# Waits of a two-block network on one core: orders of exponentials, scaled keys, tables, scalings and norms changed

## Chip, cores and metric

One core of a Trainium2 chip. The metric is the device time of one execution in microseconds, the median of several runs; the profile comes from one further execution.

## What is computed

Two blocks of two layers each, width 1024, 256 tokens (the first block has a second sequence of 256 context tokens), all in float32. The output is that of the last layer of the second block. Cut to what matters:

```python
# first block, layer 0 (even) and 1 (odd)
h = h + 0.5 * m[2] * swiglu(modulate(rmsnorm(h)), ffn1)     # 1024 -> 2 x 2816 -> 1024
h = h + m[5] * mixer(modulate(rmsnorm(h)))   # layer 0: wkv scan in both directions; 1: depthwise conv 31 + pools
h = h + 0.5 * m[8] * swiglu(modulate(rmsnorm(h)), ffn2)
# the scan of layer 0, for both sequences and both directions
sk = S @ kk[t]; S = S * w[t] - sk b[t]^T + v[t] k[t]^T; y[t] = S @ r[t]
# second block: layer_norm(alpha * x + (1 + gate) * f(modulate(x))), f = swiglu, mixer, swiglu
# mixer of layer 0: RG-LRU (linear recurrence over time) beside gated linear attention in chunks of 64
# mixer of layer 1: latent attention
cq, ckv, k_pe = split(u @ w_in); q = rms_norm(cq) @ w_q_up; kv = rms_norm(ckv) @ w_kv_up
q_pe, k_pe = rope(q_pe), rope(k_pe); o = softmax(causal(q k^T)) v; return o @ w_out
```

## The kernel before

All five engines run one long program each, written out by hand; semaphores tie them together. Activations lie as columns of features by 256 tokens (X, Y), weights come in chunks of 256 columns into two buffers W[0] and W[1] (SyncE issues their transfers; `free(c)` waits until chunk c-2 has been used), and products go to four PSUM banks in turn, each of which ScalarE or VectorE must empty (semaphore `s_ev`) before it is used for the fourth tile after. `phases` gives the order of stages: the first FFN F[0], the rwkv mixer, F[1], F[2], the conv mixer, F[3], F[4], the gated linear attention ("gla"), F[5], F[6], the latent attention ("mla"), F[7], with norms between them.

**FFNs F[1] to F[7]** (`small_ffn`, one on each engine) do each pair of 2 x 128 gate and up columns as seven products of half size (L2522; the down columns L2562) instead of eight, with sums of weight blocks (S1 to S4: L2841, L2846, L2850, L2855) and of token blocks (L2864 to L2871) on VectorE. In a pair u ScalarE copies the first product to C1 (L2641), which TensorE's second product in the same banks waits for, takes the silu S0 (L2645) and, when VectorE has the sum, the silu C12 (L2647). In F[4] to F[7] ScalarE runs `norm_scale` (L1555, eight activations on X) at the start of u=1; VectorE waits for it (`s_xa`) before the down columns. Before F[1] ScalarE takes the silu of the rows c (CB, L2711), which VectorE needs for the modulation products (`ada`, L2754), in F[1] from pair 2 on; VectorE waits for it (`s_sc` 4) before the token sums of F[1].

**The scan of rwkv** (`rwkv_scan_pe`, `_act`, `_dve`, `_pool`) takes chunks n = 0 to 3 for one sequence and 4 to 7 for the other; the heads are in two halves t = 0, 1. Within a chunk a chain of small products (64 x 64) goes back and forth between TensorE and the engines that empty and mask its banks. For the next chunk ScalarE computes exponentials (`exps`, L861 to L864, and `inverse_exps`, L873, into KH), GpSimd multiplies them with keys (`keys`, L1136 and L1139; `inverse_keys`, L1146 and L1147, into BH and KH), TensorE forms `first_b` (L654) and `first_a` (L640, L643) and VectorE masks them (L1022, L1017). ScalarE's order in a chunk: the copies of turned keys KHT and BHT (L907, L908) for t=0 and 1, the copies VT1 and VT0 of turned values (L911, L915) for t=0 and 1, then `inverse_exps` for t=0 and 1, then the copies GG and UU1 (L877). TensorE's: turned values (L664), Q2 products, then for each t the product that needs VT0 and, where there is a next chunk, its `first_b`; then for each t the product with GG and `first_a`. In the second sequence VectorE does bonus products (L1076 to L1079) before it masks `first_b`.

**Conv and gla.** `first` makes SyncE wait (conv: for the end of the FFN before; gla: for the last modulation group) and issue five transfers of small tables (conv: the pool weights, L1334, and the pool table, 1 MB, L1336; gla: L1544, L1545) before the first weights of the mixer (L2364). In the gla mixer VectorE needs, for the recurrence (L1814) the factor TH (1 + TH, L1803, reciprocal, L1804, product, L1805, then ScalarE's Sqrt, L1745) and, for the attention, the scaled QD, KI and KE (L1807 to L1809), without which TensorE's `scores` (L1613) don't start. After them come SCO cleared (L1810), AI (L1812), the recurrence, the masks (L1822), the copies KET (L1828) and the states (L1833 to L1836).

**The mla mixer** projects to three tiles of latents CQ and one of keys KP (L604, copies L2024, L2026), squares the three (L2029), sums them (L1926), takes two roots (L2032), reciprocals (L2094) and norms (L2097), and multiplies up (L1941 queries, L1951 and L1956 keys and values). The angles' sine tables (L2052, L2053) come after the value copies, and VectorE waits for them before the rotation (L2103 to L2116).

## Time and profile before

| | |
|---|---|
| runs | 3156.06 us median of 3 (3154.03, 3156.06, 3161.24) |
| profiled execution | 3164.83 us, its span 3163.0 us |
| busy | PE 2955.0 us, VectorE (DVE) 1886.0, ScalarE (ACT) 566.5, GpSimd (POOL) 221.4 |
| mean granted clock of TensorE | 0.972 |
| rwkv mixer | about 522 to 1050 us; hand-overs to a next chunk at about 617 to 628, 653 to 664, 688 to 700, 861 to 873, 902 to 914, 945 to 956 |
| conv, gla, mla mixers | from 1502, 2082 and 2794 us |

PE is TensorE's products, PEld its loads of weights, SPq SyncE's queue of transfers. A row of a timeline gives start, duration, engine, line of the kernel, operation, tiles written and read, shapes and count; in brackets the idle time of the engine before it and what ended it. "Granted clock" is the share of 2.4 GHz that the chip let TensorE have: 1.00 is 2.4 GHz, 0.50 is 1.2 GHz. A float32 product shows as two MATMUL rows.

### The profile page before, as it was taken

The page shows a single profiled execution, that of the slowest core. Times are in us where ns is not written, and L with a number is a line of the kernel's source. Part 1 is how long each engine was busy: PE and PEld are TensorE (multiplying, and loading weights), DVE is VectorE, ACT ScalarE, POOL GpSimd, SP SyncE. Part 2 cuts the span into 40 slices and gives each one's busy share as a digit, 9 for nine tenths or more (in the row PEclk, how much of TensorE's full clock was granted, in tenths as well). Part 3 has the DMA queues.
Part 4 walks back from the last instruction along what each step waited for, and adds up shares of the span by engine and source line. Part 5 has one row for each costly group of instructions (what it writes and reads, how often), then busy time and mean ns, then how long its engine had stood idle before and what let it go on. Part 6 is the DMA issues. An engine that isn't in the chain of part 4 may idle for free.

```text
span 3163.0 us, 60794 instructions
## 1 busy us (share of the span) xinstructions
PE 2955.0 (93%) x26672; PEld 2528.8 (80%) x26672; DVE 1886.0 (60%) x3357; ACT 566.5 (18%) x1281; POOL 221.4 (7%) x363
## 2 busy tenths in 40 slices
PE   7999999879888999999989999999989989989998
PEld 5444445777787899999789999977889989967998
DVE  6646666645455586786638768635237667623664
ACT  2000002434332100100320011024111020031201
POOL 0000000432331000000000000000000000000000
PEclk8999999999999999999999999999999999998999
DMA  8678994102202466564435646533335535522452
GB/s 307 239 258 313 367 366 159 42 4 81 68 4 96 134 218 217 190 226 150 133 123 197 223 164 213 187 111 110 119 122 164 194 110 162 183 72 75 129 189 90
DMA packets 365169, 514.84 MB, mean 163 GB/s; under 512 B 11552, under 2 KB 342496, under 8 KB 357104
## 3 DMA queue, kind: packets, MB, share of 16 engines
q1 hardware_dynamic: 347632, 366.73, 35.6%
q0 software_dynamic: 17136, 144.19, 11.6%
q8 instruction: 206, 3.38, 0.5%
q14 instruction: 51, 0.42, 0.0%
q10 hardware_dynamic: 144, 0.13, 0.0%
HBM read 509.97 MB, written 1.05 MB: 162 GB/s over the span
## 4 chain that ended last, share of the span: by engine, by line
PE 83%; DVE 5%; DMA 5%; ACT 4%; issue 2%; POOL 1%; SPq 0%; DVEq 0%; ACTq 0%; POOLq 0%
PE PS L2522 29%; PE PS L2562 15%; PE PS L2452 7%; PE PS L604 6%; PE PS L2472 5%; PE PS L624 5%; PE PS L780 3%; PE PS L1678 2%; PE PS L1603 2%; PE PS L2573 2%; DMA ADAW<-in_ada_rows 2%; DMA W<-in_ffn_w_down 1%; DVE ADAW L2754 1%; PE PS L1362 1%; PE PS L2430 1%
## 5 line engine op out<-in xcount | busy, mean ns | idle before, releaser
L2522 PE MATMUL PS<-Y,W 128*128 128x128 f32 x4928 | 596.2, 280 | 42.5 <-ACT Y L2675 31.2
L2522 PEld LDWEIGHTS PS<-Y,W 128*128 128x128 f32 x4928 | 580.0, 196 | 47.8 <-issue 33.9
L2522 PE MATMUL PS<-Y,ARENA 128*128 128x128 f32 x3696 | 439.0, 275 | 0.0
L2522 PEld LDWEIGHTS PS<-Y,ARENA 128*128 128x128 f32 x3696 | 426.3, 192 | 0.0
L2452 PE MATMUL PS<-Y,W 128*128 128x512 f32 x704 | 305.4, 597 | 2.2 <-ACT Y L2675 2.2
L2562 PE MATMUL PS<-ARENA,W 128*128 128x128 f32 x2464 | 286.5, 275 | 8.0 <-DVE ARENA L2870 4.8
L2562 PEld LDWEIGHTS PS<-ARENA,W 128*128 128x128 f32 x2464 | 280.1, 192 | 9.9 <-DVE ARENA L2870 6.5
L2452 PEld LDWEIGHTS PS<-Y,W 128*128 128x128 f32 x704 | 134.7, 192 | 172.1 <-issue 172.1
L2754 DVE SCALAR_TENSOR_TENSOR ADAW<-ADAW,CB 128x1024 f32<-128x1024 f32 x208 | 246.5, 1221 | 16.7 <-DMA ADAW<-in_ada_rows 16.3
L2472 PE MATMUL PS<-ARENA,W 128*128 128x512 f32 x352 | 151.3, 592 | 1.2 <-DVE ARENA L2818 1.2
L2841 DVE TENSOR_TENSOR ARENA<-W 128x1024 f32<-128x1024 f32 (+1 forms) x105 | 139.4, 1328 | 12.5 <-DMA W<-in_ffn_w_down 5.4
L2562 PE MATMUL PS<-ARENA 128*128 128x128 f32 x1232 | 146.7, 275 | 0.0
L604 PE MATMUL PS<-Y,W 128*128 128x256 f32 (+2 forms) x560 | 128.7, 394 | 18.3 <-ACT Y L2675 8.7
L2562 PEld LDWEIGHTS PS<-ARENA 128*128 128x128 f32 x1232 | 142.1, 192 | 0.0
L2846 DVE TENSOR_TENSOR ARENA<-ARENA,W 128x1024 f32<-128x1024 f32 (+1 forms) x105 | 139.1, 1325 | 0.2
L604 PEld LDWEIGHTS PS<-Y,W 128*128 128x128 f32 (+2 forms) x560 | 108.3, 194 | 38.6 <-issue 10.1
L2850 DVE TENSOR_TENSOR W<-W 128x1024 f32<-128x1024 f32 (+1 forms) x105 | 139.1, 1325 | 0.0
L2647 ACT ACTIVATE SIL<-SIL 128x256 f32<-128x256 f32 x77 | 32.1, 417 | 584.3 <-DVE SIL L2913 584.3
L2472 PEld LDWEIGHTS PS<-ARENA,W 128*128 128x128 f32 x352 | 66.8, 190 | 85.7 <-issue 83.5
L780 PE MATMUL PS<-Y,W 128*128 128x256 f32 x528 | 124.0, 394 | 9.9 <-ACT Y L2675 4.6
L624 PE MATMUL PS<-W 64*64 64x64 f32 x4608 | 111.1, 222 | 20.2 <-issue 17.1
L780 PEld LDWEIGHTS PS<-Y,W 128*128 128x128 f32 x528 | 102.5, 197 | 31.4 <-issue 13.7
(403 smaller groups left out, 3704.0 us busy)
## 6 DMA issues: line engine op xcount, KB each, us to landing
ADAW<-in_ada_rows POOLq DMA_DIRECT2D x52, 2048.0 KB, 8.1
W<-in_ffn_w_gu SPq DMA_DIRECT2D x88, 1024.0 KB, 7.7
W<-in_ffn_in SPq DMA_DIRECT2D x88, 1024.0 KB, 7.6
W<-in_ffn_w_down SPq DMA_DIRECT2D x32, 1408.0 KB, 11.2
W<-in_ffn_out SPq DMA_DIRECT2D x32, 1408.0 KB, 9.4
ADAW<-in_ada_rows POOLq DMA_DIRECT2D x64, 512.0 KB, 6.6
W<-in_even_w_in SPq DMA_DIRECT2D x40, 512.0 KB, 4.7
W<-in_e_w_in SPq DMA_DIRECT2D x16, 512.0 KB, 4.4
```

Source lines behind the costliest of these rows:

```text
L604: last = mm(PS[idx % 4][0:m_, 0:S], wide(c, kt, n_)[:, k, q * P:q * P + m_], x(k), start=(k == 0), stop=(k == kt - 1))
L624: last = mm(to, x, y, start=(k == 0), stop=(k == len(pairs) - 1))
L780: last_ = mm(PS[at[f] % 4][:, 0:S], w[:, k, q * P:(q + 1) * P], Y[:, k, off:off + S], start=(k == 0), stop=(k == DT - 1))
L1603: last = mm(PS[idx % 4][:, 0:S], wide(c, DT)[:, k, (i % 2) * P:(i % 2 + 1) * P], Y[:, k, 0:S], start=(k == 0), stop=(k == DT - 1))
L2452: last = mm(o, gate_up(c)[:, g, k, q * P:(q + 1) * P], Y[:, k, 0:T], start=(k == 0), stop=(k == DT - 1))
L2472: last = mm(PS[idx % 4][:, 0:T], wide(c, FT)[:, k, q * P:(q + 1) * P], H[:, k, 0:T], start=(k == 0), stop=(k == FT - 1))
L2522: last = mm(block_bank(b, q), w[left][:, k, q * P:(q + 1) * P], YB[right][:, k], start=(k == 0 and p not in (2, 5)), stop=(k == 3), skip_g ...
L2562: last = mm(block_bank(b, 0), w[left][:, k], HB[right][:, k], start=(k == 0 and p not in (2, 5)), stop=(k == PAIRS - 1), skip_group_check= ...
L2754: ins = V.scalar_tensor_tensor(w, w, 1.0, c_rows, ALU.mult, ALU.mult, accum_out=MOD[:, layer, tile + i:tile + i + 1])
L2841: V.tensor_tensor(w["S1"], w["A21"], w["A22"], ALU.add).then_inc(s_s1, 1)
L2846: V.tensor_tensor(w["S2"], w["S1"], w["A11"], ALU.subtract).then_inc(s_s2, 1)
L2850: V.tensor_tensor(w["S3"], w["A11"], w["A21"], ALU.subtract).then_inc(s_s3, 1)
```

## The change

Nothing is computed otherwise, except that single instructions are cut into parts; the orders are changed:

- rwkv, ScalarE: `inverse_exps(t)` comes just before the wait for VT of the same half.
- conv and gla, SyncE: the tables' wait and transfers come after the second weight chunk of the mixer.
- gla, VectorE: the reciprocal is cut in two halves of four tiles; the scaled keys come between them; AI and the recurrence come after the KET copies, the recurrence in two halves behind the states of heads 0 and 1.
- mla, ScalarE: the sines come right after `norm_scale`, with one small Sqrt behind them; each latent tile is squared from its bank right after its copy, and the wait of TensorE for the common square goes. VectorE norms the two query tiles first, then the key tile, each after its own root; TensorE waits for the second before the key products.
- F[4] to F[7], ScalarE: `norm_scale` goes in four parts of two tiles behind S0 of the pairs 1 to 4.
- F[1]: ScalarE's silu of CB goes behind S0 of pair 0; VectorE's wait for it to the start of pair 1.

The diff, cut to its core:

```diff
@@ -907,6 +907,9 @@
                 for t in range(NT):
+                    if more:
+                        inverse_exps(t, n + 1)
                     act.wait_ge(s_pp[t], e_pe.after(n, "VT"))
@@ -914,9 +917,6 @@
                     ins.then_inc(s_va[t], 1)
-                if more:
-                    for t in range(NT):
-                        inverse_exps(t, n + 1)
                 for t in range(NT):
@@ -1335,7 +1335,7 @@
-            m["pin"]["first"] = first
+            m["pin"]["after"] = {1: first}
             m["phases"] = conv_phases
@@ -1544,21 +1544,22 @@
-            m["p1"]["first"] = first
+            m["p1"]["after"] = {1: first}
             m["phases"] = gla_phases
...
-        def norm_scale(A, n_xa):
+        def norm_scale(A, n_xa, tiles=range(DT)):
...
             g, b = x_scales[n_xa]
-            for j in range(DT):
+            for j in tiles:
                 ins = A(X[:, 0, j], X[:, 0, j], ACT.Identity, bias=0.0 if b is None else b[:, j:j + 1], scale=g[:, j:j + 1])
-            ins.then_inc(s_xa, 1)
+            if tiles[-1] == DT - 1:
+                ins.then_inc(s_xa, 1)
...
             n_y, n_xa = n["y"], n["xa"]
-            n_sp, n_xc, n_sp2, n_l, n_den, n_ls, n_be, n_th, n_qk = [bump("x") for _ in range(9)]
+            n_sp, n_xc, n_sp2, n_l, n_den, n_ls, n_be, n_qk, n_th = [bump("x") for _ in range(9)]
             e_done, ln_done, squared = 1, 2, 11
@@ -1801,18 +1802,22 @@
                 link(V.tensor_scalar(YH, TH, 1.0, None, ALU.add))
-                link(V.reciprocal(YH, YH))
-                say(V.scalar_tensor_tensor(TH, TH, 2.0, YH, ALU.mult, ALU.mult), n_th)
+                h0, h1 = slice(0, DT // 2), slice(DT // 2, DT)
+                link(V.reciprocal(YH[:, h0], YH[:, h0]))
                 dve.wait_ge(s_ga, 9)
...
                 link(V.memset(SCO, 0.0))
-                dve.wait_ge(s_ga, 10)
-                link(V.tensor_tensor(AI, AI, TH, ALU.mult))
-                for f in range(DT):
-                    ins = V.tensor_tensor_scan(XC[:, f], AR_[:, f], AI[:, f], 0.0, ALU.mult, ALU.add)
-                link(ins)
+                link(V.reciprocal(YH[:, h1], YH[:, h1]))
+                say(V.scalar_tensor_tensor(TH, TH, 2.0, YH, ALU.mult, ALU.mult), n_th)
+                def recurrence(fs):
+                    for f in fs:
+                        ins = V.tensor_tensor_scan(XC[:, f], AR_[:, f], AI[:, f], 0.0, ALU.mult, ALU.add)
+                    link(ins)
                 dve.wait_ge(s_gm, 1)
@@ -1826,6 +1831,8 @@
                     V.tensor_copy(KET[:, tt], gbank(G_KET + tt)[:, :]).then_inc(s_ge, 1)
+                dve.wait_ge(s_ga, 10)
+                link(V.tensor_tensor(AI, AI, TH, ALU.mult))
                 for h in range(4):
@@ -1835,6 +1842,8 @@
                                            ALU.add).then_inc(s_ge, 2)
+                    if h < 2:
+                        recurrence(range(4 * h, 4 * h + 4))
                 for i in range(DT):
@@ -1906,7 +1915,7 @@
             n_y, n_xa = n["y"], n["xa"]
-            n_ang, n_lat, n_rope, n_rest = [bump("x") for _ in range(4)]
+            n_ang, n_lat, n_lat2, n_rope, n_rest = [bump("x") for _ in range(5)]
             order = ["s0", "s1"]
@@ -1919,7 +1928,6 @@
                 idx = m["nrm"]
-                pe.wait_ge(s_ma, 1)
                 pe.wait_ge(s_ev, idx)
@@ -1945,6 +1953,7 @@
                 pe.wait_ge(s_w[c % 2], 32 * (c // 2 + 1))
+                pe.wait_ge(s_xr, n_lat2)
                 wk = wide(c, 1, 2048)[:, 0].rearrange("p (h two n) -> p h two n", h=NH, two=2)
@@ -2017,16 +2026,20 @@
                 norm_scale(A, n_xa)
+                act.wait_ge(s_xr, n_ang)
+                A(COS[0:HD], COS[0:HD], ACT.Sin)
+                A(SIN[0:HD], SIN[0:HD], ACT.Sin).then_inc(s_ma, 1)
+                A(ANG[0:HD, 2, 0:1], eps["one"][0:HD], ACT.Sqrt)
                 idx = m["p1"]["t0"]
...
                     if i < 3:
-                        A(CQ[:, i], PS[idx % 4][:, 0:S], ACT.Copy).then_inc(s_ev, 1)
+                        A(CQ[:, i], PS[idx % 4][:, 0:S], ACT.Copy)
+                        A(SQM[:, i], PS[idx % 4][:, 0:S], ACT.Square).then_inc(s_ev, 1)
                     else:
...
                     idx += 1
-                act.wait_ge(s_ev, idx)
-                A(SQM, CQ, ACT.Square).then_inc(s_ma, 1)
                 for g in range(2):
@@ -2048,9 +2061,7 @@
                     idx += 1
-                act.wait_ge(s_xr, n_ang)
-                A(COS[0:HD], COS[0:HD], ACT.Sin)
-                A(SIN[0:HD], SIN[0:HD], ACT.Sin).then_inc(s_ma, 1)
                 def exps(h):
@@ -2090,13 +2101,14 @@
-                dve.wait_ge(s_ev, m["up"]["t0"])
-                link(V.reciprocal(ANG[:, 0:2], ANG[:, 0:2]))
-                for i in range(3):
-                    g = vec("q_norm_g_2", i) if i < 2 else vec("kv_norm_g_2", 0)
-                    ins = V.scalar_tensor_tensor(CQ[:, i], CQ[:, i], g, ANG[:, i // 2], ALU.mult, ALU.mult)
-                say(ins, n_lat)
-                dve.wait_ge(s_ma, 2)
+                for g, tiles, k in ((0, (0, 1), n_lat), (1, (2,), n_lat2)):
+                    dve.wait_ge(s_ev, m["up"]["t0"] - 1 + g)
+                    link(V.reciprocal(ANG[:, g], ANG[:, g]))
+                    for i in tiles:
+                        ins = V.scalar_tensor_tensor(CQ[:, i], CQ[:, i], vec("kv_norm_g_2", 0) if g else vec("q_norm_g_2", i),
+                                                     ANG[:, g], ALU.mult, ALU.mult)
+                    say(ins, k)
+                dve.wait_ge(s_ma, 1)
                 idx = m["rot"]
@@ -2633,8 +2645,6 @@
                 for u in range(PAIRS):
-                    if u == 1 and n_xa:
-                        norm_scale(A, n_xa)
                     fd = fd0 + 5 * u
@@ -2643,6 +2653,11 @@
                     A(halves(S0), both_banks(BX), ACT.Silu).then_inc(s_fa, 1)
+                    if n_xa and 1 <= u <= 4:
+                        norm_scale(A, n_xa, range(2 * u - 2, 2 * u))
+                    if u == 0 and sec["i"] == 0:
+                        act.wait_ge(s_c2, 48)
+                        A(CB[:, :], CB[:, :], ACT.Silu).then_inc(s_sc, 1)
                     act.wait_ge(s_fd, fd + 5)
@@ -2706,9 +2721,6 @@
                 elif ph[0] == "small":
-                    if ph[1] == 1:
-                        act.wait_ge(s_c2, 48)
-                        A(CB[:, :], CB[:, :], ACT.Silu).then_inc(s_sc, 1)
                     small_ffn(F[ph[1]], ph[3])
@@ -2873,8 +2885,7 @@
                 g = sec["group0"]
-                if i == 0:
-                    dve.wait_ge(s_sc, 4)
+                assert not sec["groups"][0]
@@ -2883,6 +2894,8 @@
                     more = sec["groups"][u]
+                    if u == 1 and i == 0:
+                        dve.wait_ge(s_sc, 4)
                     if u:
```

## Rows read from the trace of the kernel before

**Rows 1.** The page of the profile: shares of the chain that ended last, by engine.

```profile
PE 83%; DVE 5%; DMA 5%; ACT 4%; issue 2%; POOL 1%; SPq 0%; DVEq 0%; ACTq 0%; POOLq 0%
```

**Rows 2.** Groups of instructions by line and form, 590 to 1000 us: busy, mean, idle before.

```profile
L654 PE MATMUL PS<-W 64*64 64x64 f32 x384 | 18.5, 261 | 22.2 <-POOL W L1147 20.2 <-ACT ARENA L949 1.9
```

**Rows 3.** Timeline, first and fourth hand-over of the scan: start, us, engine, line, [idle before].

```profile
616.40 0.48 ACT L908 ACTIVATE ADAW<-PS 128x384 f32<-128x384 f32 x1
...
619.12 1.32 ACT L915 ACTIVATE ADAW<-PS 64x192 f32<-64x192 f32 x4
...
620.47 1.13 ACT L873 ACTIVATE W<-ARENA 128x192 f32<-128x192 f32 x4
621.16 0.59 POOL L1146 TENSOR_TENSOR W<-ARENA,W 128x192 f32<-128x192 f32 x1 [7.31 <-ACT W L873]
...
625.64 0.92 PE L654 MATMUL PS<-W 64*64 64x64 f32 x24 [0.58 <-POOL W L1147]
...
865.24 0.71 POOL L1146 TENSOR_TENSOR W<-ARENA,W 128x192 f32<-128x192 f32 x1 [5.62 <-ACT W L873]
```

**Rows 4.** Windows: PE, PEld, DVE, ACT, POOL busy (count), then the granted clock.

```profile
660.00:663.00 3.00, 3.00 (x86) 3.00 (x84) 0.56 (x1) 0.49 (x1) 2.45 (x4) 0.50 0.02 5
...
835.00:998.00 163.00, 135.76 (x4816) 126.29 (x4816) 95.83 (x202) 58.76 (x162) 55.41 (x88) 0.98 0.03 10
2195.00:2198.00 3.00, 3.00 (x12) 2.73 (x13) 2.97 (x4) 0.00 (x0) 0.00 (x0) 0.50 0.02 5
...
2851.00:2855.00 4.00, 4.00 (x12) 2.40 (x11) 3.12 (x2) 0.00 (x0) 0.00 (x0) 0.50 0.00 0
```

**Rows 5.** Timelines, start of the second FFN (F[1]) and of the third (F[2]).

```profile
1060.42 3.82 PE L2522 MATMUL PS<-Y,W 128*128 128x128 f32 x16 [5.07 <-ACT Y L2675]
...
1064.54 1.91 ACT L2711 ACTIVATE CB<-CB 128x2048 f32<-128x2048 f32 x1
...
1077.07 0.42 DVE L2902 TENSOR_TENSOR SIL<-SIL,PS 128x256 f32<-128x256 f32 x1 [2.02 <-PE PS L2522]
...
1285.22 3.82 PE L2522 MATMUL PS<-Y,W 128*128 128x128 f32 x16 [4.37 <-ACT Y L2675]
...
1297.77 0.42 DVE L2902 TENSOR_TENSOR SIL<-SIL,PS 128x256 f32<-128x256 f32 x1 [2.02 <-PE PS L2522]
```

**Rows 6.** Timeline, start of the conv mixer.

```profile
1504.86 4.04 ACT L2675 ACTIVATE Y<-Y,MOD,GS 128x256 f32<-128x256 f32 x8 [2.62 <-DVE Y L3000]
...
1509.66 2.93 PE L604 MATMUL PS<-Y,W 128*128 128x256 f32 x6 [7.93 <-DMA W<-in_o_w_in]
```

**Rows 7.** Timeline, second pair of gate and up columns in F[4] and F[5].

```profile
1875.84 2.05 PE L2522 MATMUL PS<-Y,W 128*128 128x128 f32 x16 [0.92 <-ACT JUNK L2641]
...
2360.49 4.03 ACT L1555 ACTIVATE X<-X,VEC 128x256 f32<-128x256 f32 x8
...
2364.84 2.05 PE L2522 MATMUL PS<-Y,W 128*128 128x128 f32 x16 [1.66 <-ACT JUNK L2641]
```

**Rows 8.** Timeline, the gated linear attention around its first scores.

```profile
2174.14 12.95 DVE L1804 RECIPROCAL Y<-Y 128x2048 f32<-128x2048 f32 x1
...
2187.13 2.29 DVE L1805 SCALAR_TENSOR_TENSOR ARENA<-ARENA,Y 128x2048 f32<-128x2048 f32 x1
...
2193.01 1.97 PE L1613 MATMUL PS<-ADAW 128*64 128x64 f32 x32 [5.45 <-DVE ADAW L1809]
...
2203.14 1.29 DVE L1828 COPY ADAW<-PS 128x512 f32<-128x512 f32 x2
```

**Rows 9.** Timeline, latent attention: norms of the latents, and its rotation.

```profile
2812.49 1.56 PE L1926 MATMUL PS<-ADAW,CT 128*128 128x256 f32 x6 [1.34 <-ACT ADAW L2029]
2813.66 0.91 ACT L2032 ACTIVATE ARENA<-PS,CT 128x256 f32<-128x256 f32 x2 [1.22 <-PE PS L1926]
2814.67 3.35 DVE L2094 RECIPROCAL ARENA<-ARENA 128x512 f32<-128x512 f32 x1 [15.87 <-ACT ARENA L2032]
...
2819.39 16.32 PE L1941 MATMUL PS<-ARENA,W 128*128 128x256 f32 x64 [5.33 <-DVE ARENA L2097]
```

## The prediction

> **What bounds the kernel now.** I read the page first: TensorE carries 83% of the chain that ended last, VectorE, ScalarE and GpSimd together 10% [rows 1]. So an edit on ScalarE, VectorE, GpSimd or a queue is worth only what TensorE stands still for it, plus what its clock loses after the stop. I then went through the idle time of TensorE where the diff touches the code (groups by line, timelines), and read the granted clock in windows: 1.00 is 2.4 GHz, 0.50 is 1.2 GHz.
>
> **1. Scan (rwkv): the inverse exponentials before the VT copies.** TensorE stood idle 20.2 us before `first_b` (L654), released by the key products of GpSimd (L1147) [rows 2]; these are the six hand-overs to a next chunk (n=0,1,2 and 4,5,6; the first chunks of both sequences don't have them). In the first one [rows 3] ScalarE ends its KHT/BHT copies at 616.9, copies VT of both halves until 620.45, and only then issues L873 (4 instructions, 1.13 us); GpSimd starts at 621.16, needs 8 products of about 0.55 us, and `first_b` of the second half starts at 625.64. Moved: the exponentials of half 0 run at 616.9 to 617.5, so GpSimd scales half 0 at 617.6 to 619.8 and half 1 to 622.0. VT of half 1 ends 1.13 later, at 621.6; its product (0.75) ends at 622.35, and `first_b` of half 1 starts there: 3.3 us sooner. TensorE's old wait goes (20.2 us over six) and a new one of about 0.7 us, for VT of half 1, comes each time: 20.2 - 6 x 0.7 = 16.0. On top, after these stops the clock was 0.50 in four of the six hand-overs (the window at 660 is one [rows 4]; those at 695, 868 and 909 read the same). From window to window such stretches last 3.4, 5.4, 3.3 and 3.3 us, with TensorE busy throughout. With stops under 1 us I expect them at 1.00: half of 15.4, 7.7. Together 24. Bounds: 12 (idle alone, with twice the new wait) and 26.
> Cover: in the second sequence VectorE does bonus products (L1076 to L1079, about 2.6 us) before it masks `first_b`; they end where the earlier mask is wanted, so nothing is added, and at most 0.5 us each time if they don't.
> GpSimd's products now run beside those VectorE instructions. Where they did so already, in the fourth hand-over, the first product took 0.71 instead of 0.59 us [rows 3]. At that price three hand-overs lose some 0.4 us in all, inside the bounds. The Trainium skill (SBUF — State Buffer, Who interferes with whom) says that a VectorE instruction with two SBUF inputs and a GpSimd instruction that reads SBUF exclude each other for a whole instruction; by that rule the two bonus products of 0.7 us would be added in each of three hand-overs, and the sum would be 44 instead of 48. The 0.71 us, far from 0.59 + 0.7, speaks against that.
>
> **2. F[1] (second FFN): silu of the rows c.** A table load and L2711 (1.91 us) stand between TensorE's first product and the copy C1 that its next one waits for, and VectorE's token sums wait for it. F[2] has the same code without it. From the first product to the second sum of U3 (L2902) it takes 1077.07 - 1060.42 = 16.65 us in F[1] and 1297.77 - 1285.22 = 12.55 in F[2] [rows 5]. Gain 4.1, bounds 1.9 (the silu's length alone) and 4.1. In its new place ScalarE idles until C12 (10 us), and nobody needs CB before u=2: the added wait of VectorE at u=1 costs nothing.
>
> **3. Conv: the pool tables after chunk 1.** The first weights are now queued behind a wait for the end of F[2] and five issues; TensorE waited 7.93 us for them and started at 1509.66, while the first quarter of Y was there at 1504.86 plus two of eight activations, 1505.9 [rows 6]. Chunk 0 can load as soon as the down columns before last are used, chunk 1 when the last are; Y then decides, at 1506.1: 3.6 sooner. As the clock is low after either stop, and how much of the first tiles it takes differs by about 0.6 from start to start, I take 3.0; bounds 0 and 3.6. Past chunk 1 SyncE waits for an event that is already there by then, and the 1 MB of POOLM lies before chunk 2, which is wanted only when TensorE has done two chunks, about 14 us later. In the linear attention the same move is worth 0: there TensorE starts on Y and not on W. If that cover went, both moves would cost at most the 5 issues, about 3 us.
>
> **4. F[4] to F[7]: norm_scale split.** Eight activations (4.03 us) stood in front of C1 at u=1; TensorE waited 0.92 in F[4] and 1.66 in F[5] [rows 7], in F[6] and F[7] the same 1.66. Two activations (1.0 us) behind S0 at u=1 to 4 lie in ScalarE's wait of 7 us for C12. Gain 0.92 + 3 x 1.66 = 5.9; lower bound 4. VectorE's wait for s_xa is after u=10: still covered.
>
> **5. Linear attention: reciprocal halved, recurrence later.** VectorE's reciprocal (12.95 us) and L1805 stood before the three scaled keys; TensorE waited 5.45 us for them, until 2193.01 [rows 8]. Half a reciprocal is 6.5: the keys are ready at 2174.1 + 6.5 + 3.5 = 2184.2, and TensorE comes at 2187.6. The wait goes, and with it the low clock of 2193 to 2199 (the window at 2195 is one of it [rows 4]): 5.45 + half of 6 = 8.45. What is late next: SCO and KET. Memset 0.9, second half 6.5, L1805 2.3, masks 1.8, KET 1.3 [rows 8] end at 2197.4, and TensorE wants KET after tile 2 at 2196.6: 0.8 lost. ScalarE's root, with its two table loads, keeps ScalarE from copying tile 1 until 2197.4; that bank is wanted for tile 5 only. Gain 7.6; bounds 4.5 and 8.5.
>
> **6. Latent attention.** Squares taken tile by tile save the single Square: of the 1.34 us that TensorE waited before its sums [rows 9] the copy of the last tile (0.4) stays, so they start 0.9 sooner, at 2811.6. VectorE used to wait for both roots, take 3.35 us of reciprocal and three products, until 2819.39 [rows 9]. For the query norm alone: first sum at 2811.6 + 1.15, root 0.46, half the reciprocal 1.7, two products 0.86: 2816.0. Gain 3.4; the key norm follows 2.2 us later and is wanted after 16 tiles. The sines, with two table loads and the small Sqrt (3.5 us in all), now stand before the copy of tile 0 at 2801; TensorE has four banks, so until 2811 that is free. VectorE's wait for the sines in the rotation goes too, but TensorE's products there (3.6 us) pace it: 0, at most 2. Gain 3.4, bounds 1.5 and 6.
>
> **Sum.** 24 + 4.1 + 3.0 + 5.9 + 7.6 + 3.4 = 48 us. The profiled execution took 3164.8 (span 3163.0), the median of the runs is 3156.1, 0.3% lower; I take the 48 from either: 3117 profiled, median 3108.
>
> **Rivals.** (Chances in brackets; the forecast itself has 58%, with 3103 to 3115 as its own range.)
> - **A, the clock doesn't come back (20%).** The stops shrink, but the stretches behind them stay at 0.50, and the new VT wait is twice as long: scan 12, linear attention 4.7, the rest 16: gain 33, 3123. For it: rows at 0.50 occur with TensorE wholly busy. Against: two of the six hand-overs, with stops just as long, show 1.00.
> - **B, the attention's clock (12%).** From 2851 to 2868 TensorE was busy at 0.50 [rows 4], after 3.1 us idle. The stop there becomes a little shorter and falls elsewhere in time. If the clock holds, 8.5 us more: gain 57, 3099. Against: the stop is still about 2.9 us.
> - **C, slower (2%): the scan falls to the low clock for good.** In the attention 17 us of 64-row products did not raise it. The scan's products are of that kind; TensorE is busy 136 of 163 us in its second half [rows 4] and 111 of 141 in its first. Each microsecond of this that goes from 2.4 to 1.2 GHz costs one; from 48 such us on all the rest is eaten, at 80 it is 3188. Against: after each fall in the scan the clock was back within 6 us.
> - **D, GpSimd and VectorE shut each other out (6%).** Each bonus product of VectorE holds up a key product for its 0.7 us, two in each of three hand-overs: 4 us less, gain 44, 3112. For it only that the two now meet; against it the 0.71 us above.
> - **E, no change (2%).** The hand-overs are shorter, but TensorE meets, right after, masks or copies that don't move, and the FFN gains go to weight loads: within 6 us, 3153. Against: every wait behind the hand-over hangs on an event that moves with it.
>
> **Numbers.** Forecast and D lie between 3103 and 3115. The range reaches to A and B, with the bounds of the terms about them: 3091 to 3127; left out are C, E and the far tails of A and B. A measurement of this kernel can't tell 0.2% (6 us) from no change. Faster 0.96, the same 0.02, slower 0.02.
>
> **What would show it.** Idle before L654 on GpSimd from 20 us to under 3, L873 before L911, windows behind it at 1.00; L2711 behind L2645; first W of conv issued before L1334; idle before L2641's successor at u=1 gone; L1613 starting with no wait and a small one before L1632; L1941 3.4 us nearer to the end of L604. I am wrong if TensorE's idle in the scan doesn't fall by 10 us, if the clock is lower in the scan than 0.96 and 0.98, or if the FFNs of F[4] on become longer.

## Result and the profile of the changed kernel

The changed kernel took **3114.3 us** (median of 4 runs, 3112.1 to 3118.0) against 3155.1 us for the kernel before, run beside it: a ratio of 0.986 (95% interval 0.984 to 0.988). A later comparison with more runs (after_timed, below) gave 0.985 (0.983 to 0.987). Faster by 1.4 to 1.5%, 44 to 48 us. I had predicted 3108 (range 3091 to 3127) and a gain of 48.

The page of the changed kernel: span, busy time, and shares of the chain that ended last, which answers to [rows 1].

```profile
span 3113.6 us, 60803 instructions
...
PE 2939.6 (94%) x26672; PEld 2514.8 (81%) x26672; DVE 1887.1 (61%) x3359; ACT 567.2 (18%) x1285; POOL 223.9 (7%) x363
...
PE 86%; DVE 4%; DMA 3%; ACT 3%; issue 2%; POOL 1%; SPq 0%; DVEq 0%; ACTq 0%; POOLq 0%
```

TensorE's share of the chain went from 83% to 86%; it does the same work (26672 MATMUL rows in both) in 15 us less busy time and stands still 34 us less.

Groups of instructions by line and form, 590 to 1000 us (both scans); the first line answers to [rows 2]. The last line is the second one's counterpart in the kernel before.

```profile
L654 PE MATMUL PS<-W 64*64 64x64 f32 x358 | 13.2, 219 | 2.5 <-POOL W L1147 1.5 <-ACT ARENA L949 0.9
L624 PE MATMUL PS<-CB,W 64*64 64x64 f32 x384 | 13.0, 226 | 2.9 <-ACT ADAW L918 2.9
```
```profile
L624 PE MATMUL PS<-CB,W 64*64 64x64 f32 x384 | 15.8, 248 | 0.4 <-ACT ADAW L915 0.4
```

Before `first_b` TensorE now waits 1.5 us for GpSimd instead of 20.2. The new wait is in the second line: 2.9 us for the VT copies (L918, L915 before), where the product that reads them had to wait 0.4 us in all. These two waits together fell by 16.2 us.

Timeline of the first hand-over and of the fourth, which answers to [rows 3].

```profile
611.62 0.48 ACT L908 ACTIVATE ADAW<-PS 128x384 f32<-128x384 f32 x1
...
611.99 0.62 ACT L873 ACTIVATE W<-ARENA 128x192 f32<-128x192 f32 x2
...
612.69 0.59 POOL L1146 TENSOR_TENSOR W<-ARENA,W 128x192 f32<-128x192 f32 x1 [3.61 <-ACT W L873]
...
614.22 0.62 ACT L873 ACTIVATE W<-ARENA 128x192 f32<-128x192 f32 x2
...
615.26 1.32 ACT L918 ACTIVATE ADAW<-PS 64x192 f32<-64x192 f32 x4
...
616.57 0.60 POOL L1147 TENSOR_TENSOR W<-ARENA,W 128x192 f32<-128x192 f32 x1
...
616.72 0.34 PE L624 MATMUL PS<-CB,W 64*64 64x64 f32 x8 [0.42 <-ACT ADAW L918]
...
617.45 0.92 PE L654 MATMUL PS<-W 64*64 64x64 f32 x24
```
```profile
851.57 0.59 POOL L1146 TENSOR_TENSOR W<-ARENA,W 128x192 f32<-128x192 f32 x1
851.88 0.83 DVE L1076 TENSOR_TENSOR Y<-ARENA 128x512 f32<-128x512 f32 x1
...
852.12 1.04 POOL L1147 TENSOR_TENSOR W<-ARENA,W 128x192 f32<-128x192 f32 x1
852.74 0.96 DVE L1077 TENSOR_TENSOR Y<-Y,ARENA 128x512 f32<-128x512 f32 x1
853.12 1.04 POOL L1146 TENSOR_TENSOR W<-ARENA,W 128x192 f32<-128x192 f32 x1
...
853.37 0.34 PE L624 MATMUL PS<-CB,W 64*64 64x64 f32 x8 [0.42 <-ACT ADAW L918]
...
854.80 0.92 PE L654 MATMUL PS<-W 64*64 64x64 f32 x24 [0.51 <-POOL W L1147]
```

The exponentials of half 0 (L873) start about when the copies (L908) end, GpSimd starts 1.1 us after that copy's start instead of 4.8, and `first_b` of half 1 follows its predecessors without a stop. VT of half 1 (L918, until 616.6) is what is late next: 0.42 us. In the fourth hand-over two of the eight key products take 1.04 instead of 0.59 us, and there `first_b` of half 1 waits 0.51 us for GpSimd.

Windows of the same kernel, columns as in [rows 4]: the first scan, the second, one of the two stretches at the low clock that are left inside the scans, and the start of the attention.

```profile
592.00:722.00 130.00, 106.26 (x4208) 97.20 (x4204) 67.50 (x126) 54.66 (x148) 46.92 (x75) 0.99 0.02 4
822.00:980.00 158.00, 135.66 (x4875) 125.44 (x4875) 98.41 (x206) 58.66 (x162) 58.04 (x89) 1.00 0.03 11
702.00:706.00 4.00, 3.58 (x124) 3.58 (x126) 1.21 (x3) 0.98 (x2) 1.39 (x3) 0.57 0.02 4
2801.00:2821.00 20.00, 20.00 (x60) 13.33 (x60) 7.21 (x17) 3.23 (x15) 0.00 (x0) 0.52 0.00 1
```

Timeline of the start of F[1], which answers to [rows 5].

```profile
1037.78 3.82 PE L2534 MATMUL PS<-Y,W 128*128 128x128 f32 x16 [5.25 <-ACT Y L2690]
...
1045.25 1.90 ACT L2660 ACTIVATE CB<-CB 128x2048 f32<-128x2048 f32 x1
...
1050.40 0.42 DVE L2915 TENSOR_TENSOR SIL<-SIL,PS 128x256 f32<-128x256 f32 x1 [2.02 <-PE PS L2534]
```

From the first product to the second sum of U3 (L2915) it takes 12.62 us now, F[2]'s length to within 0.1; the silu of the rows c (L2660) stands behind S0.

Timelines of the start of conv, of the pair u=1 in F[5], of the linear attention and of the latent attention: they answer to [rows 6] to [rows 9].

```profile
1476.50 4.04 ACT L2690 ACTIVATE Y<-Y,MOD,GS 128x256 f32<-128x256 f32 x8 [2.61 <-DVE Y L3013]
...
1477.74 2.47 PE L604 MATMUL PS<-Y,W 128*128 128x256 f32 x5 [4.36 <-ACT Y L2690]
```
```profile
2323.41 1.08 ACT L1555 ACTIVATE X<-X,VEC 128x256 f32<-128x256 f32 x2
...
2324.72 1.95 PE L2534 MATMUL PS<-Y,W 128*128 128x128 f32 x16
```
```profile
2141.44 6.55 DVE L1807 RECIPROCAL Y<-Y 128x1024 f32<-128x1024 f32 x1
...
2154.78 1.15 PE L1614 MATMUL PS<-ADAW 128*64 128x64 f32 x32
...
2163.50 1.29 DVE L1833 COPY ADAW<-PS 128x512 f32<-128x512 f32 x2
...
2164.84 1.13 PE L1633 MATMUL PS<-X,ADAW 64*128 64x256 f32 x6 [0.97 <-DVE ADAW L1833]
```
```profile
2765.46 1.56 PE L1934 MATMUL PS<-ADAW,CT 128*128 128x256 f32 x6 [0.47 <-ACT ARENA L2041]
2769.93 15.91 PE L1949 MATMUL PS<-ARENA,W 128*128 128x256 f32 x64 [2.91 <-DVE ARENA L2108]
...
2800.58 0.49 PE L1990 MATMUL PS<-ARENA 128*128 128x128 f32 x2 [2.90 <-DVE ARENA L2128]
```

Conv starts on Y (1.24 us after L2690's first activation) and no longer on its weights. In F[5] two scalings (1.08 us) follow S0, and TensorE goes on without a stop. The first scores of the linear attention (L1614) start with no wait, and 0.97 us is lost before the product that reads KET (L1633). In the latent attention the stop before the query products fell from 5.33 to 2.91 us.

**By stages.** The stages lie one after the other, so each can be measured by itself from one start of TensorE to the next (the scans from their first L624 row to the next product of another part of the kernel, for the second scan the output projection L604; F[7] to its last product). Their lengths are the same in all profiles of the study to within a few tenths, except where the clock falls. The table has the means over all profiled executions in which the stage's code was the old one and over those in which it was that of the changed kernel (the last column but one: what the prediction had for it).

| stage | old code: us (profiles) | changed: us (profiles) | gain | predicted | smallest and largest gain of a pair |
|---|---|---|---|---|---|
| both scans | 320.8 (5) | 301.0 (8) | 19.9 | 24 | 15.1 to 26.1 |
| F[1] | 224.4 (4) | 219.9 (10) | 4.6 | 4.1 | 4.0 to 5.6 |
| F[2] and the start of conv | 223.7 (5) | 219.9 (9) | 3.9 | 3.0 | 2.5 to 5.0 |
| F[4] | 226.2 (4) | 225.0 (10) | 1.1 | 0.9 | 0.7 to 1.7 |
| linear attention | 260.5 (4) | 254.2 (9) | 6.3 | 7.6 | 3.4 to 9.1 |
| F[5], F[6] | 449.7 (4) | 445.5 (10) | 4.2 | 3.3 | 3.4 to 5.2 |
| latent attention | 138.8 (6) | 136.8 (6) | 2.0 | 3.4 | 1.3 to 2.9 |
| F[7] | 220.1 (4) | 218.5 (10) | 1.5 | 1.7 | 1.0 to 2.0 |

The sum is 43.5, with 48 predicted; the two timed ratios say 43.6 and 48.3.

### The profile page after: what moved, and what is told of

It reads as the page before. It is cut to its first block, busy times and chain, and to the rows that moved or that the text cites. A ratio compares the mean times of both kernels' runs of the same rounds, so it can differ in the third digit from the quotient of the medians.

```text
span 3113.6 us, 60803 instructions
## 1 busy us (share of the span) xinstructions
PE 2939.6 (94%) x26672; PEld 2514.8 (81%) x26672; DVE 1887.1 (61%) x3359; ACT 567.2 (18%) x1285; POOL 223.9 (7%) x363
## 4 chain that ended last, share of the span: by engine, by line
PE 86%; DVE 4%; DMA 3%; ACT 3%; issue 2%; POOL 1%; SPq 0%; DVEq 0%; ACTq 0%; POOLq 0%
PE PS L2534 30%; PE PS L2574 15%; PE PS L2464 10%; PE PS L604 6%; PE PS L2484 5%; PE PS L624 4%; PE PS L780 3%; PE PS L1679 2%; PE PS L2585 2%; PE PS L1604 1%; DMA W<-in_ffn_w_down 1%; PE PS L1362 1%; PE PS L1456 1%; PE PS L2442 1%; PE PS L2609 1%
## 5 line engine op out<-in xcount | busy, mean ns | idle before, releaser
L2534 PEld LDWEIGHTS PS<-Y,W 128*128 128x128 f32 x4928 | 576.8, 196 | 40.3 <-issue 34.2
L2464 PEld LDWEIGHTS PS<-Y,W 128*128 128x128 f32 x704 | 134.4, 191 | 171.3 <-issue 171.3
L2766 DVE SCALAR_TENSOR_TENSOR ADAW<-ADAW,CB 128x1024 f32<-128x1024 f32 x208 | 246.3, 1219 | 11.4 <-DMA ADAW<-in_ada_rows 10.9
L604 PE MATMUL PS<-Y,W 128*128 128x256 f32 (+2 forms) x560 | 129.3, 395 | 14.8 <-ACT Y L2690 13.1
L604 PEld LDWEIGHTS PS<-Y,W 128*128 128x128 f32 (+2 forms) x560 | 108.6, 195 | 35.4 <-issue 14.9
L624 PE MATMUL PS<-W 64*64 64x64 f32 x4608 | 113.0, 224 | 23.1 <-issue 19.6
L780 PE MATMUL PS<-Y,W 128*128 128x256 f32 x528 | 123.5, 393 | 10.1 <-ACT Y L2690 4.6
L624 PEld LDWEIGHTS PS<-W 64*64 64x64 f32 x4608 | 99.9, 136 | 34.1 <-issue 30.9
```

What stands on the lines that cost most here:

```text
L604: last = mm(PS[idx % 4][0:m_, 0:S], wide(c, kt, n_)[:, k, q * P:q * P + m_], x(k), start=(k == 0), stop=(k == kt - 1))
L624: last = mm(to, x, y, start=(k == 0), stop=(k == len(pairs) - 1))
L780: last_ = mm(PS[at[f] % 4][:, 0:S], w[:, k, q * P:(q + 1) * P], Y[:, k, off:off + S], start=(k == 0), stop=(k == DT - 1))
L2464: last = mm(o, gate_up(c)[:, g, k, q * P:(q + 1) * P], Y[:, k, 0:T], start=(k == 0), stop=(k == DT - 1))
L2534: last = mm(block_bank(b, q), w[left][:, k, q * P:(q + 1) * P], YB[right][:, k], start=(k == 0 and p not in (2, 5)), stop=(k == 3), skip_g ...
L2766: ins = V.scalar_tensor_tensor(w, w, 1.0, c_rows, ALU.mult, ALU.mult, accum_out=MOD[:, layer, tile + i:tile + i + 1])
```

## The experiments

### again_before and again_after: the two kernels profiled once more

No edit. The first pair of profiles was 49 us apart, the medians 41.

> The kernel before, profiled a second time. The two profiled executions were 49 us apart, the medians 41. If the 8 us are chance in the execution of before (its start and where the clock falls), this profile is shorter: a span of 3152 to 3157 instead of 3163, with the same waits (the idle time before first_b on GpSimd 20 us again) but fewer or shorter stretches at 0.50 or an earlier first scan. If they are not chance, it comes out at 3163 again with the stretches in the same places.

> The changed kernel, profiled a second time. In its first profile the clock fell twice in the last chunk of the first scan (at 702 and 722 us), where the kernel before had no fall until 734, and the attention stood at 0.50 for 20.5 us instead of 17. If where the clock falls is tied to the stops of the program, both come again within 1 us of their places; if it is chance of the execution, they move or go, and the scan gets shorter by up to 3 us. Span 3110 to 3116 either way.

Measured: again_before took 3157.1 us (span 3155.3), again_after 3109.4 (span 3107.6). The long waits at the six hand-overs (3.1 and 3.3 us) came again to 0.02 us, and the stops without a releaser ("issue", see below) within 3 us in sum. What moved is where the clock fell. In the first scan of the kernel before it was low at 659 and 693 us (3.4 and 6.8 us long) in one execution, at 658 and 696 (3.4 each) in the other, and in the second scan at 867, 908 and 1018 against 849, 866, 907, 948, 1000 and 1017. In the changed kernel the fall at 702 did not come again, and the one right behind the scan's end (722) came again there (718). The shorter span of again_before goes with less time at 0.50 in the whole execution (167 us instead of 181), as I had expected, but not in the scans (28 instead of 21). So the falls inside a scan change from one execution to the next; both scans together took 321.4 and 322.8 us before, 302.9 and 297.6 after. In the changed kernel the two differ by 5 us, so a single pair of profiles tells the scans' gain no better, which is why the table above goes by means.

### scan_only and rest_only: the change in two halves

scan_only is the kernel before with this edit; rest_only is the changed kernel with it undone.

```
@@ rwkv_scan_act, the loop over chunks @@
                 for t in range(NT):
+                    if more:
+                        inverse_exps(t, n + 1)
                     act.wait_ge(s_pp[t], e_pe.after(n, "VT"))
...
-                if more:
-                    for t in range(NT):
-                        inverse_exps(t, n + 1)
```

> Only the scan's part of the change on the kernel before. My step 1 said 24 us. Theory P (the prediction's sizes): 3131. Theory Q (waits as predicted, but the clock gives less and TensorE's unexplained stops grow, as the first profile of the changed kernel reads): 18.5 us, 3136.5, both scans together 303 us long instead of 321. Theory R (the two key products that take 1.04 instead of 0.59 us beside VectorE's bonus products set the pace in the second sequence): the second sequence gains less than 3 us per hand-over while the first gains 3.5.

> The change with the scan as before. By the prediction's sum 24 us remain of 48 (3131); by the stages of the first profile pair, without what lies before the scans, about 24 too, of which the latent attention gives 2.0. If the parts depend on each other (through where the clock falls), the gains of this kernel and of scan_only together differ from the 41 us of the whole by more than 4 us; if not, this one gives 41 less what scan_only gives, 3133 to 3137.

Measured: scan_only 3132.9 us, ratio 0.992 (0.991 to 0.994), a gain of 25 us (21 to 29); rest_only 3132.8, ratio 0.992 (0.991 to 0.994), 25 us too. For the whole, the changed kernel was timed again in more rounds (after_timed: 3112.6 us against 3160.1). I had put on record before it: 46 to 52 us if the parts don't depend on each other, 38 to 43 if they take from each other. It gave 48, against 50 for the two halves, each with some 4 us of uncertainty, so the parts don't depend on each other much. In the profile of scan_only both scans together took 296.8 us, the shortest of all, in rest_only 321.3. The timed value sides with theory P, the scans' mean over eight profiles (19.9) with theory Q; the runs don't tell 20 from 24 here. Theory R was wrong as put: the second sequence gained 13.7 of the 24.6 us by which scan_only's scans are shorter than those of the first profile of the kernel before, no less than the first sequence.

**Where the rest of the 24 went.** In the profiles with the old scan code the clock is at 0.50 for 20 to 31 us inside the two scans, in those with the new one for 3 to 12. That is 18 us less on average, and half of it, 9, is what I would have counted. TensorE's busy time in the scans fell by 6.0 (means 265.5 and 259.5), a third of the 18. TensorE also has stops that the profile puts down to nothing ("issue"), mostly three or four in a chunk. They stand at fixed places of the instruction stream: in before, after and again_after most fall on the same MATMUL rows, counted from the first scan's start, and within a chunk they are mostly 126 or 127 rows apart. They come to 26.0 to 29.0 us in the scans of the old code (mean 27.2) and to 26.7 to 31.2 in those of the new (29.4). The largest group of them, by line and form, 590 to 1025 us, in again_before and then in again_after:

```profile
L624 PE MATMUL PS<-W 64*64 64x64 f32 x4608 | 112.4, 224 | 19.8 <-issue 16.9 <-DVE X L1107 1.6 <-DVE W L1017 0.3
```
```profile
L624 PE MATMUL PS<-W 64*64 64x64 f32 x4608 | 111.3, 222 | 20.6 <-issue 17.3 <-DVE X L1107 1.6 <-DVE W L1017 0.7
```

This group holds 16.9 and 17.3 us of "issue". In the first profile of the changed kernel, whose scans were among the longest of the new code (302.9 us), it holds 19.6:

```profile
L624 PE MATMUL PS<-W 64*64 64x64 f32 x4608 | 113.0, 224 | 23.1 <-issue 19.6 <-DVE X L1107 1.6 <-DVE W L1017 0.7
```

So the 19.9 us are: 16.1 of waits with a releaser (27.0 to 10.9 on average, with 16.0 predicted), and 6.0 of busy time less the 2.2 of these stops, 4 where I had 7.7. What the "issue" stops are wasn't tried; that they lie at fixed places and don't get shorter when the products get faster is what the traces show.

### bonus_late: do VectorE's bonus products slow GpSimd's key products?

```
@@ rwkv_scan_dve @@
+                if more:
+                    for t in range(NT):
+                        first_b(t, n + 1)
                 if lat and n - n0 < 3:
                     two = slice(2 * (n - n0), 2 * (n - n0) + 2)
...
-                if more:
-                    for t in range(NT):
-                        first_b(t, n + 1)
```

> The changed kernel with VectorE's bonus products behind the two masks of first_b, so that they no longer run beside GpSimd's key products. Theory V (the two key products of 1.04 instead of 0.59 us are slow because VectorE's products with two inputs in SBUF run beside them): all eight take 0.59 again, the wait of 0.51 us before first_b of half 1 goes in each of three hand-overs, and the second scan is up to 1.5 us shorter, less what the masks of first_a lose by the bonus products of 2.6 us ahead of them (0 to 1 us each). Theory W (the 1.04 has another cause): two products stay at 1.04 and the wait stays. The whole is within 3 us of the changed kernel either way.

The instructions of L1146 on GpSimd in the second scan (count, then shortest, median and longest in ns), first of the changed kernel (its profile in after_timed), then of bonus_late:

```profile
L1146 POOL TENSOR_TENSOR W<-ARENA,W x12: 588/593/1038, 852.5 to 931.9; 128x192 f32<-128x192 f32 x12
```
```profile
L1146 POOL TENSOR_TENSOR W<-ARENA,W x12: 582/593/597, 855.2 to 936.1; 128x192 f32<-128x192 f32 x12
```

Theory V holds: the longest fell from 1038 to 597 ns, and the wait before `first_b` is gone. But the kernel took 3120.1 us, ratio 0.987 (0.985 to 0.989), some 7 us slower than the changed kernel by the medians (the two intervals overlap), and the second scan 179.5 us instead of 173.2 in after_timed and 169.9 to 174.1 in all eight profiles with the changed scan. Behind the masks the bonus products hold up those of `first_a`:

```profile
865.74 0.93 PE L624 MATMUL PS<-ADAW 64*64 64x64 f32 x48 [0.86 <-DVE W L1017]
```

Such a stop comes in each of the three hand-overs (2.6 us in all, against 1.5 saved at `first_b`), the "issue" stops are 2.0 us longer, and the clock was low for 13.7 us in this scan instead of 6.8. The stops at the masks are inside the 0 to 1 us each that I had allowed; that the whole stays within 3 us of the changed kernel was wrong, and what was missing is the clock and the "issue" stops. Why these two grew isn't shown. So the rival D's mechanism is real, but its price is 0.51 us in each of three hand-overs, about the 0.5 that I had allowed for cover, and the place that the change leaves to the bonus products is the better one.

In the fourth hand-over two key products take 1.04 us each beside L1076 (0.83) and L1077 (0.96), and the VectorE instructions are longer as well: these two took 0.68 and 0.69 in the kernel before. The rows shown above look like turns: L1146 ends at 852.16, L1076 0.55 us later, L1147 0.45 after that, L1077 0.54 after that and the next L1146 0.46 after that. Each instruction ends 0.45 to 0.55 us after the one on the other engine, somewhat less than its undisturbed length (0.59 and 0.7), and since it had begun before that, only 0.45 us is added to a key product. The Trainium skill (SBUF — State Buffer, Who interferes with whom) calls the ports that VectorE and GpSimd share an exclusive lock, and says that a VectorE instruction with two SBUF inputs contends there with a GpSimd instruction that reads SBUF. The trace fits that better than I had thought from the 0.71 us of [rows 3]; what doesn't come is the whole VectorE instruction (0.7) that I had added to each product by that rule.

### mla_undone: what the latent attention's part is worth

The changed kernel with `mla_phases` as before (the edit is that part of the change, undone).

> The changed kernel with the latent attention as before. Theory P (the prediction): 3.4 us slower than the changed kernel. Theory U (the shorter stop before the query products, 2.9 instead of 5.3 us, moves the attention's stretch at 0.50 from 17 to 20.5 or 24 us, as three profiles with and three without this part read): the stop costs 2.4 + 0.9 us, the stretch comes back to 17 and gives 1.7 to 3.4 us, so it is 0 to 2 us slower than the changed kernel.

Measured: 3116.9 us, ratio 0.986 (0.984 to 0.989), against 3112.6 and 0.985 (0.983 to 0.987) for the changed kernel in the same comparison. The two medians are 4 us apart and can't tell the theories from each other. The stage can, since with the same code its length is the same to within 0.9 us (138.5 to 139.3 in six profiles with the old code, 136.5 to 137.2 in six with the new). In us, from the stage's first product:

| kernels | to the norm sums | to the query products | to the first scores | attention | all | clock low in the attention |
|---|---|---|---|---|---|---|
| old code (6 profiles) | 18.1 to 18.6 | 6.9 | 31.1 to 31.4 | 41.3 to 41.4 | 97.4 to 98.3 | 17.1 |
| changed (after, after_timed, rest_only) | 17.7 | 4.5 | 30.7 | 43.0 | 95.8 | 20.5 |
| changed (again_after, gla_whole, bonus_late) | 16.1 to 16.3 | 4.5 | 30.4 to 32.0 | 43.6 to 44.4 | 95.4 to 96.1 | 23.9 |
| rot_early | 17.6 | 4.5 | 31.0 | 33.6 | 86.6 | 0 |
| rot_first | 17.7 | 4.5 | 29.1 | 33.6 | 84.8 | 0 |

Theory U holds, at the upper end of its 0 to 2 us. Everything ahead of the attention came 3.3 us sooner or more (56.1 to 56.9 us before the first scores with the old code, 52.8 in the next three and 51.0 to 52.5 in the three after them), as predicted (3.4). Then the attention itself, whose code didn't change, took 1.6 to 3.0 us more, because the clock stayed at 0.50 for 20.5 or 23.9 us instead of 17.1. Net 2.0. The stop before the scores hardly changed (3.08 to 2.90 us), and no run tells what made the stretch longer: 17.1 in all six profiles of the old code, 20.5 or 23.9 in all six of the new.

### rot_early and rot_first: what brings on the low clock in the attention

rot_early moves TensorE's value products behind the rotation products; rot_first moves the rotation products ahead of the key products too. ScalarE's counts and the weight buffer's last use move with them.

```
@@ mla_phases, pe, the value products (for tt) and the rotation products (for g in range(4)) @@
-                for tt in range(2):
-                    for g in range(2):
...
                 pe.wait_ge(s_ev, idx)
                 for g in range(4):
...
+                pe.wait_ge(s_ev, idx)
+                for tt in range(2):
+                    for g in range(2):
...
@@ act @@
                     if i < 8:
                         A(KN[:, i], PS[idx % 4][:, 0:S], ACT.Copy).then_inc(s_ev, 1)
+                        if i == 7:
+                            idx += 5
```

> The changed kernel, with the rotation products of the latent attention moved ahead of the four value products, so that VectorE rotates beside these. TensorE's stop of 2.9 us before the first scores goes (the values are 3.6 us long, the rotation after its last product takes 3.3), and new stops of about 0.4 us come before and after the values. Theory S (that stop brings on the stretch at 0.50 of 17 to 24 us at the attention's start): the stretch falls to 7 us or less, and the time by 2 + 5 to 8 = 7 to 10 us. Theory T (the attention's own small products, which wait for maxima and exponentials, keep the clock low whatever comes before): the stretch stays at 17 to 24 us and the gain is 2 us.

> The changed kernel with the rotation products ahead of both the key and the value products (rot_early has them between the two). Theory S (a long stop before the attention brings on its low stretch): here too no stop ahead of the scores is longer than 0.8 us, so the stretch is 7 us or less, and the time is that of rot_early within 1.5 us, 6 to 9 less than the changed kernel. If it was the accident of where rot_early's stops fell, the stretch is 17 us or more and the gain 2 us.

Measured: rot_early 3105.6 us, ratio 0.983 (0.981 to 0.984); rot_first **3100.2 us, ratio 0.982 (0.981 to 0.984)**, the fastest of the study, 8 us below the changed kernel by the ratios. The rows, first of the kernel before, then of rot_early, then of rot_first: the stops before the moved products and before the first scores (L1981, L1990, L1992).

```profile
2850.64 0.51 PE L1981 MATMUL PS<-ARENA 128*128 128x128 f32 x2 [3.08 <-DVE ARENA L2116]
```
```profile
2794.58 5.40 PE L1975 MATMUL PS<-W,ARENA 128*128 128x512 f32 x8 [0.67 <-DVE ARENA L2121]
2800.76 0.46 PE L1990 MATMUL PS<-ARENA 128*128 128x128 f32 x2 [0.78 <-ACT ARENA L2063]
```
```profile
2787.96 3.72 PE L1971 MATMUL PS<-ARENA,W 128*128 128x256 f32 x16 [0.68 <-DVE ARENA L2122]
...
2795.89 0.46 PE L1992 MATMUL PS<-ARENA 128*128 128x128 f32 x2 [0.78 <-ACT ARENA L2064]
```

The stop of 2.90 us before the scores became 0.78. Windows over the attention, columns as in [rows 4]: the changed kernel at its start and behind it, then rot_first over its first 32 us.

```profile
2823.00:2843.00 20.00, 18.83 (x108) 14.37 (x108) 8.61 (x29) 5.53 (x22) 0.00 (x0) 1.00 0.00 0
```
```profile
2791.00:2823.00 32.00, 31.22 (x161) 21.47 (x160) 13.72 (x41) 12.18 (x40) 0.00 (x0) 1.00 0.10 33
```

The window of the changed kernel from 2801 to 2821 (above) holds 60 MATMUL rows in 20 us at a clock of 0.52, with TensorE busy all the time. From 2823 to 2843 it has 108 rows of the same kind at 1.00, with TensorE busy 94% of the time; rot_first has 161 in 32 us at 1.00 from the values on. Theory S holds, and further than I had written: the stretch didn't shrink to 7 us, it went (in rot_early the clock fell for 3.4 us at 2794.6, behind a stop of 0.67, and was back before the scores). The attention takes 33.6 us instead of 41.3 to 44.4. One thing the two edits don't separate: both shorten the stop, and both put the value products (128 rows) directly ahead of the scores, where the rotation products (64 rows) had been. No run shortened the stop and left that order, so what is shown is that the two together remove the stretch. In these traces the attention's products keep the clock up once it is up, and leave it down for 17 to 24 us once it is down, although the engine is then busy without a gap. The Trainium skill (TensorE: Matmul & The Clock Gate, What's actually happening) says that the clock is set by how busy the engine has been recently, with the low one as the default. The traces agree as to what comes before the scores; that the engine shows as busy for all of 20 us at 0.50 doesn't go with it, and none of my runs tells what of these products the gate counts.

### ffn_only, gla_only, gla_whole: the FFNs and the linear attention

ffn_only and gla_only are the kernel before with those parts of the change alone. gla_whole is the changed kernel with this edit:

```
@@ gla_phases, dve @@
-                link(V.reciprocal(YH[:, h0], YH[:, h0]))
+                link(V.reciprocal(YH, YH))
...
-                link(V.reciprocal(YH[:, h1], YH[:, h1]))
```

> Only the two FFN parts on the kernel before: the norm scalings in pairs of tiles, and the silu of the rows c behind the first S0 of F[1]. The prediction's terms: 4.1 + 5.9 = 10.0 us. The stage lengths of the changed kernel's profiles against those of before read 4 to 5 in F[1] and 1.2, 2.4, 2.6 and 1.0 in F[4] to F[7]: 11 to 12. If the clock after these stops changes too, up to 14; if the wait in front of C1 only moves to another stop in the same pair of columns, under 4.

> Only the linear attention's part on the kernel before. The prediction: 7.6 us (bounds 4.5 and 8.5). The idle time of 5.5 us before the first scores goes, and a new one of 0.8 us comes before the product that reads KET. If the stretch at 0.50 behind the first scores comes back elsewhere, 4.7.

> The changed kernel with VectorE's reciprocal in one piece again, and all else (the product with TH behind the keys, the recurrence late) as changed. Theory H (the halving does most): the keys come 6.5 us later than in the changed kernel, TensorE waits about 3.2 us for them (5.45 less the 2.3 us of the product with TH that no longer lies ahead) with a low clock behind it (up to 3 us), and 0.8 is saved at KET: 3 to 5.5 us slower than the changed kernel. Theory O (the order does most): less than 2 us slower.

Measured: ffn_only 3145.6 us, ratio 0.997 (0.996 to 0.998), a gain of 10.1 us (7 to 14); by its stages F[1] gave 4.9 and F[4] to F[7] 7.5. gla_only 3148.3, ratio 0.998 (0.997 to 0.999), 5.4 us (2.5 to 8.2); its stage took 252.8 instead of 260.5, 7.7 less. Both are as predicted (10.0 and 7.6), within what the timing can tell. gla_whole took 3112.4 us, ratio 0.987 (0.985 to 0.988), which with 0.985 for the changed kernel leaves it open whether it is slower at all. Its stage answers more sharply: 256.0 us against 253.8 to 253.9 in six profiles of the changed code (256.3 in again_after and 255.5 in bonus_late, where the clock fell once more, and 252.8 in gla_only). The wait is there:

```profile
2153.32 1.15 PE L1614 MATMUL PS<-ADAW 128*64 128x64 f32 x32 [3.13 <-DVE ADAW L1811]
```

It is 3.13 us (I had expected 3.2), and the wait of 0.97 us for KET is gone: 2.16 net, just the 2.2 by which the stage is longer. So of the 6.3 to 7.7 us that the part gives, the halving gives 2.2 and the order the rest: the product with TH and the recurrence behind the keys. That lies between my two theories; H was wrong in the low clock that it wanted behind the wait, which did not come (the stretches behind the first scores were gone in both). The two moves of tables (conv, linear attention) weren't run by themselves; for conv's there are the stop at its start (7.93 to 4.36 us) and the stage's length.

## Why the prediction was right, and where it was off

The predicted direction, the time and the list of waits held; 3114.3 lies 6 us above the 3108. That the sum came out within 5 us by the stages (43.5 of 48) is in part luck: three terms were too large by 6.8 together, three too small by 2.4. Point by point:

1. **Scan, 24 predicted, 20 by the profiles, 25 by the timed part alone.** The waits went as worked out: 20.2 to 1.5 for GpSimd, and a new one for VT of half 1, 0.42 each instead of 0.7, with 0.51 more in each hand-over of the second sequence; 16.0 predicted, 16.2 measured. The mis-sized number is the clock's 7.7. I took the four low stretches of one profile as bound to their stops and counted half of each (the second, read as 5.4 us, is 6.8 long, from 693.8 to 700.6). In five profiles of the same code they come to 20 to 31 us at changing places, and 3 to 12 remain in the changed code. The 18 us less gave a third, 6.0 us of busy time, and the stops without a releaser took back 2.2. That left about 4. Rival A (the clock doesn't come back) was wrong in its main point: the stretches behind the hand-overs went.
2. **F[1], 4.1 predicted, 4.6.** The comparison with F[2] was the right measure: 12.62 us against F[2]'s 12.55. The rest lies with the low clock at the stage's start, 13.7 us long in the first profile of before and 6.8 in that of the changed kernel.
3. **Conv, 3.0 predicted, 3.9.** TensorE starts 1.24 us after Y's first activation, as worked out. I had taken 0.6 off for the clock behind the stop, and it went the other way: the stretch there was 6.8 us once and 10.2 four times with the old code, and 3.4 or 6.8 with the new.
4. **norm_scale, 5.9 predicted, 6.9.** All four stops went and nothing came in their place. The sizes by stage (1.1, 1.9, 2.3, 1.5) are the stops with 0.2 to 0.6 more in F[4] to F[6].
5. **Linear attention, 7.6 predicted, 6.3 by the means and 7.7 in gla_only.** The wait of 5.45 went, the new one before KET is 0.97 instead of 0.8, and the low clock behind the first scores is gone. The clock falls once more elsewhere in the stage in some executions, which costs 1.7 to 2.4.
6. **Latent attention, 3.4 predicted, 2.0.** The 3.4 are there, ahead of the attention. I weighed rival B (the attention's clock stays up) and put the other side nowhere: that the stretch at the low clock can also get longer, which the sum had at nothing. The stretch grew from 17.1 to 20.5 or 23.9 us and took 1.6 to 3.0 back. Rival B was wrong for this change and right in size for what rot_early and rot_first do: 8.5 predicted, 7.7 measured between the old code's attention and theirs.

Rival C (the scan falls to the low clock for good) had nothing for it: both scans ran at 0.99 and 1.00 in the windows above. Its premise was also off: the attention's products are of 128 rows and 64 (L1981 is 128*128), not of the scan's kind. Rival D is real and small (bonus_late). Rival E didn't occur. What the timed median says beyond that, 41 us in the first comparison and 48 in the second, is the spread of the executions: those of the kernel before ran from 3152 to 3166 us over the study.

## What to carry to other kernels

When the bounding engine waits for a chain across three engines, look at the order on the engine in the middle: work that nobody waits for, ahead of work that somebody does, costs its whole length, and moving it costs only what is late next (here some 20 us for an edit of three lines). Read the clock's share from several profiles, never from one, and don't count half of each low stretch (here it was a third). And look at the stop ahead of a phase of small products by itself: here filling 2 us of a stop with independent work of the same engine took away over 20 us at the low clock and 9.4 us of time (43.0 to 33.6), more than shortening the chain before it gave (2.0).

## What the runs showed of the hardware that I had not expected

- The low clock can hold for 17 to 24 us with TensorE shown busy without a gap, in products of 128 rows or 64 that run at 1.00 without trouble once the clock is up (60 MATMUL rows in 20 us at 0.52, then 108 in 20 us at 1.00). It came in each of the twelve profiles with a stop of 2.9 to 3.1 us ahead, and in neither of the two with one of 0.78 and the value products before it.
- The same program's clock falls at different places in a scan from one execution to the next (20 to 31 us in all for the same code), while its falls at the long stops between stages, and in the attention, come at the same places each time.
- A GpSimd product of 0.59 us took 1.04 beside VectorE products with both inputs in SBUF, which were longer too (0.83 and 0.96 instead of 0.7). No idle time shows for it: the wait is inside the instructions' own lengths, and each ended 0.45 to 0.55 us after the other engine's.
- TensorE's stops without a releaser in code of many small products (29 us in two scans of 301) stand on the same rows of the instruction stream in different executions and kernels, mostly 126 or 127 MATMUL rows apart within a chunk, and don't shrink when the waits around them do.
- In the scans 18 us less at 0.50 took 6.0 us off TensorE's busy time, a third and not half.
